# Prompt tiles' residual sums moved to ScalarE and GpSimd, prompt picks moved to rounds 11 to 14, weight loads placed behind the exchange, in a two-layer diffusion backbone

## The reference

```
mod = silu(cond) @ w_ada + b_ada                 # shift, scale, gate, twice; one row for prompt, one for sample
h   = rmsnorm(x) * (1 + sc1) + sh1
mix = [latent attention | gated conv | chunked gating MLP](h) @ w_out
x   = x + g1 * mix                               # the residual sum of this study
h   = rmsnorm(x) * (1 + sc2) + sh2
aff = softmax(h @ w_router)                      # 16 experts
gates, idx = top_k(aff.T, 2 * n / 16)            # each expert picks 32 prompt and 128 sample tokens
x   = x + g2 * scatter_add(gates * swiglu_expert(h[idx]))
```

## Time and profile before

| | us |
|---|---|
| median of 3 runs | 2421.12 (2415.95 to 2424.13) |
| the profiled execution, device time | 2425.75 |
| its span, first to last instruction | 2424.0 |
| PE busy | 2295.1 (95%) |
| DVE busy | 783.2 (32%) |
| ACT busy | 514.2 (21%) |
| POOL busy | 380.1 (16%) |
| mean granted TensorE clock | 0.969 of full |

### The profile page before, as it was taken

How to read it: one execution, slowest core, us unless ns; L and a number is a source line. 1 busy time by engine, 2 the same in 40 slices (tenths; PEclk the granted TensorE clock), 3 DMA queues, 4 the chain that set the end, 5 groups by cost and what they waited for, 6 DMA issues and landing times.

```text
span 2424.0 us, 29991 instructions
## 1 busy us (share of the span) xinstructions
PE 2295.1 (95%) x12052; PEld 1496.4 (62%) x12052; DVE 783.2 (32%) x1444; ACT 514.2 (21%) x1050; POOL 380.1 (16%) x540
## 2 busy tenths in 40 slices
PE   6999989989998899999999999899999959999996
PEld 4545545555545787887865455456554447887785
DVE  2401245444237312111234012456533461211213
ACT  3310122222234200110033101223223330010012
POOL 3000010011000322322310000120000022332221
PEclk8999999999999899999999999999999969999998
DMA  9100168778355788988970002685642258898898
GB/s 337 35 0 22 44 162 175 159 160 184 111 181 194 266 282 280 287 289 283 335 239 27 15 7 74 142 195 126 135 124 88 86 212 286 282 284 282 281 290 308
DMA packets 217657, 440.71 MB, mean 182 GB/s; under 512 B 33665, under 2 KB 76857, under 8 KB 217569
## 3 DMA queue, kind: packets, MB, share of 16 engines
q1 hardware_dynamic: 169200, 360.28, 46.7%
q0 software_dynamic: 24560, 54.57, 9.6%
q10 hardware_dynamic: 23808, 24.66, 4.9%
HBM read 339.34 MB, written 47.65 MB: 160 GB/s over the span
## 4 chain that ended last, share of the span: by engine, by line
PE 86%; DMA 6%; DVE 4%; SPq 2%; ACT 1%; issue 1%; ACTq 0%; DVEq 0%; POOLq 0%
PE PS L1417 11%; PE PS L1249 11%; PE PS L1424 11%; PE PS L1446 9%; PE PS L1031 9%; PE PS L1181 6%; PE PS L985 6%; PE PS L1124 5%; PE PS L972 5%; DMA r<-ring 4%; PE PS L1136 3%; PE PS L1440 2%; PE PS L1085 1%; SPq L563 1%; PE PS L939 1%; DMA ring<-in_w_down_dram 1%
## 5 line engine op out<-in xcount | busy, mean ns | idle before, releaser
L1417 PEld LDWEIGHTS PS<-r,ring 128*128 128x128 f32 x2048 | 285.5, 192 | 20.1 <-issue 18.3
L1417 PE MATMUL PS<-r,ring 128*128 128x160 f32 x2048 | 287.8, 302 | 4.8 <-ACT r L1737 3.8
L1249 PE MATMUL PS<-ring,mix 128*128 128x512 f32 x640 | 287.8, 597 | 0.0
L1424 PE MATMUL PS<-r,ring 128*128 128x160 f32 x2048 | 283.4, 299 | 0.0
L1424 PEld LDWEIGHTS PS<-r,ring 128*128 128x128 f32 x2048 | 279.9, 190 | 0.0
L1446 PE MATMUL PS<-ring,r 128*128 128x512 f32 x496 | 221.1, 599 | 0.0
L1031 PE MATMUL PS<-r,ring 128*128 128x512 f32 (+1 forms) x576 | 208.4, 521 | 1.6 <-ACT r L1538 1.6
L1124 PE MATMUL PS<-lat,r 128*128 128x512 f32 (+1 forms) x416 | 190.3, 593 | 7.7 <-ACT ring L1600 5.0
L1249 PEld LDWEIGHTS PS<-ring,mix 128*128 128x128 f32 x640 | 116.9, 190 | 128.1 <-issue 127.9
L1181 PE MATMUL PS<-r 128*128 128x256 f32 x768 | 177.0, 388 | 15.2 <-DMA r<-ring 15.2
L1181 PEld LDWEIGHTS PS<-r 128*128 128x128 f32 x768 | 149.4, 195 | 50.8 <-DMA r<-ring 18.0
(11 more groups left out here) (306 smaller groups left out, 2236.3 us busy)
## 6 DMA issues: line engine op xcount, KB each, us to landing
ring<-in_w_gate_dram SPq DMA_DIRECT2D x32, 2048.0 KB, 10.3
ring<-in_w_up_dram SPq DMA_DIRECT2D x32, 2048.0 KB, 10.1
ring<-in_w_down_dram SPq DMA_DIRECT2D x31, 2048.0 KB, 9.2
ring<-in_w_ada_dram SPq DMA_DIRECT2D x15, 2048.0 KB, 10.4
r<-ring SPq DMA_DIRECT2D x144, 96.0 KB, 5.5
r<-r SPq DMA_DIRECT2D x128, 96.0 KB
r<-r ACTq DMA_DIRECT2D x128, 96.0 KB
r<-ring ACTq DMA_DIRECT2D x112, 96.0 KB, 5.0
```

The costliest lines, as they stand in the source:

```text
L1249: ins = pe.matmul(psum(2 * (s % 2) + n, 512), mix[:, k, tile * P:(tile + 1) * P], W_OUT[n][:, k, :], start=(k == 4), stop=(k == 3))
L1417: ins = pe.matmul(PS[:, b // 2, (b % 2) * 256:(b % 2) * 256 + SLOTS], W_G[:, k, b * P:(b + 1) * P], XST[par][:, k, :], start=(k == 0), sto ...
L1424: ins = pe.matmul(PS[:, 2 + b // 2, (b % 2) * 256:(b % 2) * 256 + SLOTS], W_U[:, k, b * P:(b + 1) * P], XST[par][:, k, :], start=(k == 0), ...
```

## The change

Six edits, made together:

1. SP in the attention: the exchange of an item is issued first, then the weights of piece i+2, then its bias.
2. The prompt tiles' residual sums leave DVE. ACT copies each half of the projection from PSUM into `XO` (`copy_prompt_sums`), POOL multiplies it by the gate and adds the old rows (`add_prompt_residual`: four operations of 128x512 for each tile, each waiting for the one before).
3. Prompt picks in rounds 11 to 14 (`PROMPT_ROUND = 11`), and other places for the small prompt steps between the rounds.
4. The prompt tables are read by DVE after round 15 and not after round 12, so `idx_q` (and POOL's `XQ` gathers) come after the sample's last round. The semaphore `ptab_turned` is merged into `top_turned`.
5. `XQ_BANK = (0, 2, 4, 6)`: each of the four transposed prompt tiles has its own two PSUM banks, PE no longer waits for ACT between them, and the merge's last matmuls write banks 4 to 7.
6. The final load of the two prompt tiles moves from SP's queue to POOL's, straight behind the last prompt scatter.

```diff
-PROMPT_ROUND = 8
-XQ_BANK = (4, 6, 2, 4)
+PROMPT_ROUND = 11
+XQ_BANK = (0, 2, 4, 6)
...
+                    exchange(n, (0, 1) if n < NI - 1 else range(4))
                     if i >= 0:
                         load_ada_weights(i + 2)
-                    exchange(n, (0, 1) if n < NI - 1 else range(4))
-                    if i >= 0:
                         load_ada_bias(i + 2)
...
-            sp.wait_ge(yp_added, 16 * E * DEPTH + 16)
-            load_final(0)
...
+                def add_prompt_residual(s):
+
+                    pool.wait_ge(xd_landed[s % 2], at(l, 16 * NT // 2, 16 * (s // 2 + 1)))
+                    pool.wait_ge(xo_ready, at(l, NT, s))
+                    for n in range(2):
+                        c = slice(512 * n, 512 * (n + 1))
+                        pool.wait_ge(po_copied, at(l, 2 * PT, 2 * (s - NT + PT) + n + 1))
+                        pool.tensor_tensor(XO[s % 2][:, c], XO[s % 2][:, c], g1[:, 0, c], ALU.mult).then_inc(pool_own, 1)
+                        pool.wait_ge(pool_own, at(l, 4 * PT, 4 * (s - NT + PT) + 2 * n + 1))
+                        ins = pool.tensor_tensor(XO[s % 2][:, c], XO[s % 2][:, c], XD[s % 2][:, c], ALU.add)
+                        ins.then_inc(pool_own, 1)
+                    pool.wait_ge(pool_own, at(l, 4 * PT, 4 * (s - NT + PT) + 4))
+                    pool.sem_inc(xo_ready, 1)
...
+                    pool.wait_ge(yp_added, 16 * E * DEPTH + 16)
+                    pool.dma_start(mix_flat[:, 0:D * PT].rearrange("p (t d) -> p t d", t=PT),
+                                   x_dram[0:PT * P, :].rearrange("(t p) d -> p t d", p=P)).then_inc(fx_landed[0], 16)
...
                 def turn_prompt_rows(q):
                     pe.wait_ge(xq_landed[q], at(l, 16, 16))
-                    if q == 0:
-                        pe.wait_ge(h2_ready, at(l, 2 * NT, 2 * NT))
-                    if q == 1:
-                        pe.wait_ge(ptab_ready, at(l, 1, 1))
                     if q == 2:
-                        pe.wait_ge(xo_ready, at(l, NT, NT))
-                    if q == 3:
-                        pe.wait_ge(xsp_ready, at(l, 3, 1))
+                        pe.wait_ge(route_ready, at(l, 1, 1))
...
+                def copy_prompt_sums(s):
+
+                    act.wait_ge(xo_stored[s % 2], at(l, 16 * NT // 2, 16 * (s // 2)))
+                    act.wait_ge(h2_turned, at(l, NT, s - 1))
+                    act.wait_ge(xn2_ready, at(l, NT, s - 1))
+                    for n in range(2):
+                        act.wait_ge(out_summed, at(l, 2 * NT, 2 * s + n + 1))
+                        act.activation(XO[s % 2][:, 512 * n:512 * (n + 1)], psum(2 * (s % 2) + n, 512), ACT.Copy)\
+                            .then_inc(po_copied, 1)
...
-                add_residual(NT - 2)
                 dve.wait_ge(afft_ready, at(l, len(ROUTED), 4))
-                rounds(0, 2, 2 * E)
+                rounds(0, 3, 2 * E)
                 normalise_sums(NT - 2)
-                rounds(2, 4, 2 * E)
+                rounds(3, 5, 2 * E)
                 row_maxima(NT - 2)
-                add_residual(NT - 1, 0, D // 2)
+                rounds(5, 6, 2 * E)
                 affinity(NT - 2)
-                rounds(4, 5, 2 * E)
-                add_residual(NT - 1, D // 2, D)
-                rounds(5, PROMPT_ROUND - 1, 2 * E)
+                rounds(6, 9, 2 * E)
                 normalise_sums(NT - 1)
+                rounds(9, 10, 2 * E)
                 row_maxima(NT - 1)
                 largest(PROMPT_ROUND - 1, 2 * E)
                 affinity(NT - 1)
...
-                rounds(PROMPT_ROUND + 4, PROMPT_ROUND + 5, 2 * E)
-                dve.wait_ge(ptab_turned, at(l, 1, 1))
+                rounds(PROMPT_ROUND + 4, 16, 2 * E)
+                dve.tensor_scalar(top_f[0:2 * E, CAP_P:SLOTS], top_i[0:2 * E, CAP_P:SLOTS], half_base[:, :], None, ALU.add)\
+                    .then_inc(top_ready, 1)
+                dve.wait_ge(top_turned, at(l, 4, 1))
                 dve.tensor_copy(idx_q[:, :], PS[:, 7, 0:4])
                 dve.tensor_scalar(idx_p[:, :], PS[:, 7, 16:16 + E], 4.0, jcol[:, :], ALU.mult, ALU.add)
                 dve.tensor_copy(gate_p[:, :], PS[:, 7, 32:32 + E]).then_inc(ptab_ready, 1)
-                rounds(PROMPT_ROUND + 5, 16, 2 * E)
...
```

More of the change, by code:

```diff
@@ L377, in backbone @@
         p_turned = sem("p_turned")
+        po_copied = sem("po_copied")
         pt_landed = [sem(f"pt_landed{i}") for i in range(2)]
@@ L404, in backbone @@
         top_turned = sem("top_turned")
-        ptab_turned = sem("ptab_turned")
+        pool_own = sem("pool_own")
         ptab_ready = sem("ptab_ready")
@@ L779, in _ @@
                 spread_inverses(NI - 1)
+                def add_prompt_residual(s):
[10 more added lines that the diff above has]
+                    pool.sem_inc(xo_ready, 1)
+                for s in range(NT - PT, NT):
+                    add_prompt_residual(s)
                 pool.wait_ge(ptab_ready, at(l, 1, 1))
@@ L1335, in prompt_tables @@
                                         start=True, stop=True)
-                    ins.then_inc(ptab_turned, 1)
+                    ins.then_inc(top_turned, 1)
                 unit_landed(l, "out0")
@@ L1394, in _ @@
                     .then_inc(top_turned, 1)
+                pe.wait_ge(h2_ready, at(l, 2 * NT, 2 * NT))
+                pe.wait_ge(ptab_ready, at(l, 1, 1))
                 pe.wait_ge(lists_ready, at(l, 2, 2))
@@ L1398, in _ @@
                     for j in range(4):
-                        ins = pe.matmul(PS[32 * j:32 * j + 32, g, 64:64 + E], ident[own, own], merge[own, 1, :],
+                        ins = pe.matmul(PS[32 * j:32 * j + 32, 4 + g, 64:64 + E], ident[own, own], merge[own, 1, :],
                                         start=True, stop=True)
@@ L1403, in _ @@
                 turn_prompt_rows(1)
-                pe.wait_ge(route_ready, at(l, 1, 1))
                 turn_prompt_rows(2)
-                pe.wait_ge(xsp_ready, at(l, 3, 2))
                 turn_prompt_rows(3)
@@ L1721, in _ @@
                         normalise_prompt_sums(s - 1)
+                    if NT - PT <= s < NT:
+                        copy_prompt_sums(s)
                     if s < NT:
@@ L2074, in affinity, with add_residual @@
                     dve.tensor_scalar(out, logit[:, i, :], pinv[:, i:i + 1], None, ALU.mult).then_inc(aff_ready, 1)
[L2076 to L2091, removed]
+                def add_residual(s):
+                    dve.wait_ge(out_summed, at(l, 2 * NT, 2 * s + 2))
+                    dve.wait_ge(xd_landed[s % 2], at(l, 16 * NT // 2, 16 * (s // 2 + 1)))
+                    if s >= 2:
+                        dve.wait_ge(xo_stored[s % 2], at(l, 16 * NT // 2, 16 * (s // 2)))
+                        dve.wait_ge(ss2_ready, at(l, NT, s - 1))
+                        dve.wait_ge(h2_turned, at(l, NT, s - 1))
+                    step(dve.tensor_tensor(XO[s % 2], psum_wide(2 * (s % 2), D), g1[:, 1, :], ALU.mult))
+                    dve.tensor_tensor(XO[s % 2], XO[s % 2], XD[s % 2], ALU.add).then_inc(xo_ready, 1)
                 def normalise_sums(s):
@@ L2166, in _ @@
                 dve.tensor_copy(gate_p[:, :], PS[:, 7, 32:32 + E]).then_inc(ptab_ready, 1)
-                rounds(PROMPT_ROUND + 5, 16, 2 * E)
-                dve.tensor_scalar(top_f[0:2 * E, CAP_P:SLOTS], top_i[0:2 * E, CAP_P:SLOTS], half_base[:, :], None, ALU.add)\
-                    .then_inc(top_ready, 1)
-                dve.wait_ge(top_turned, at(l, 3, 1))
+                dve.wait_ge(top_turned, at(l, 4, 2))
                 dve.tensor_copy(lists[:, :, :], PS[:, 0, 0:4 * E].rearrange("p (v e) -> p v e", v=2)).then_inc(lists_ready, 1)
                 dve.wait_ge(lists_ready, at(l, 2, 1))
-                dve.wait_ge(top_turned, at(l, 3, 2))
+                dve.wait_ge(top_turned, at(l, 4, 3))
                 dve.tensor_tensor(gate_s[:, :], lists[:, 0, 0:E], PS[:, 1, 0:E], ALU.max)
@@ L2181, in _ @@
                 dve.tensor_scalar(idx_s[:, :], merge[:, 1, :], float(NP), None, ALU.add)
-                dve.wait_ge(top_turned, at(l, 3, 3))
-                dve.tensor_scalar(idx_4[:, 0:E, :], PS[:, 0:4, 64:64 + E].rearrange("p g e -> p e g"), 4.0, jcol[:, :],
+                dve.wait_ge(top_turned, at(l, 4, 4))
+                dve.tensor_scalar(idx_4[:, 0:E, :], PS[:, 4:8, 64:64 + E].rearrange("p g e -> p e g"), 4.0, jcol[:, :],
                                   ALU.mult, ALU.add).then_inc(route_ready, 1)
```

## The result

The changed kernel takes 2441.99 us (median of 9 runs, 2438.77 to 2447.76), the kernel before in the same job 2424.13. The ratio is 1.0073, 95% interval 1.0052 to 1.0094: **slower by 0.7%**, where I forecast 1.1% faster. The profiled execution has a span of 2445.3 us against 2424.0.

The account below looks back on a forecast made before the run. PE holds most of the span's end, so gains come only where PE waits. -35.5 + (0.9 + 4.5) + (0.9 + 3.5) - 1.5 = -27.2, span 2396.8, median 2394 us; range 2379 to 2410 (8 in 10).

Parts of the forecast that it names:

- Edit 1, -35.5: Attention: PE's waits for exchanged blocks and slow matmuls behind them go, 28.5 us in layer 0, 7.0 in layer 1; bounds 28, 38.
- Does all of it go?: Attention: step arguing from item 11, where blocks already precede 2 MB of weights without such a wait, that 35.5 us go.
- stays in part, at the second prompt exchange or by new waits: Rival, attention: the exchange's wait stays in part, half of 35.5 us, giving 2411 us; chance 0.05.
- Layer 1's 7.0: Attention, layer 1, first two pieces: waits of 1.31 and 2.82 us, plus 1.8 and 1.1 of slow matmuls, gained.
- the cover of 26 us: Attention: weights come some 6 us later, but their piece is multiplied over 26 us away, so PE does not wait.
- Edits 2 and 3, +0.9 a layer: Routing: with sums moved to ACT and POOL, DVE's last round ends 0.9 us later; bounds 4.6 earlier, 7.1 later.
- 785.2 + 8p: Routing: time in us when the last round ends; p is one POOL operation, taken as 1.1 us, giving 794.0.
- 14.6 + 4p: Routing: time in us from tile 8's root to tile 9's, with p one POOL operation, taken as 1.1 us.
- the rival with 1.87: Rival, routing: DVE holds POOL off, an operation takes 1.87 us, gathers at their ceiling: 2411 us in all; chance 0.14.
- Edit 4, +4.5 and +3.5: Last round to first expert: prompt gathers issued later make the expert start 4.5 us later in layer 0, 3.5 in layer 1.
- 2 to 5 late: Layer 0, before the first expert: the last late piece makes the merge start 2 to 5 us late; POOL's queue hides 2.4.
- half of its 7.9: Final load: the bound of -4 us, if its transfer beside the stores takes half of 7.9 us; -1.5 was taken.

Follow-up runs that it names:

- The form with late weights: The kernel before with edits 3 and 4, sums kept on DVE, and SP held until DVE begins round 11 before the late weights: 2427.01 us, single run.
- after_half_pool: The changed kernel without the multiplication by the gate, so POOL does two operations for each prompt tile and not four: 2427.89 us, single run.
- after_e1_item1: The changed kernel with the weights ahead of the exchange again at item 0 alone: 2417.03 us, ratio 0.9971 to the kernel before.

## Why the prediction was wrong

- **Edit 1, -35.5, measured -3.4 in the two profiles and nothing alone (ratio 1.0006).** The step that failed is "Does all of it go?", in two sentences. "The next item's blocks stand behind those 2 MB in the new order as they do there" took items 11 and 13, which are sample items with blocks of 1536 bytes, for the prompt items. And "only one of the two 2 MB loads is now ahead of it", at "7 us a load", counted every load as 7 us wherever it stands. The runs show that the place matters: the first load used to run at 312 GB/s in a gap and cost the exchange nothing. Turned behind the first exchange, it falls into a stretch of 8 us in which it moves at 32 GB/s, and is still in front of item 1's blocks; the next load then runs into item 2's. With item 0 alone left as it was, edit 1 gains 1.06%, 25.7 us. I had named the place as the tight one, and as a rival ("stays in part, at the second prompt exchange or by new waits") with a chance of 0.05 and half the gain. It took all.
- The price of the waits was right in layer 0 and not in layer 1. With the weights first at item 0 alone layer 0 gives 25.6 of its 28.5. Layer 1's 7.0 were read off one execution: the old order takes 225.9 to 226.5 us there in six other traces, the new one 226.4, so there was nothing to gain, and my lower bound of 28 for both would not have held (25.7 by the ratio). Waits for weights at the piece, which I excluded by the cover of 26 us, did not come.
- **Edits 2 and 3, +0.9 a layer, measured +5.2 and +4.8.** The mechanism was right, its size off. By 785.2 + 8p, p = 1.26 gives 795.3, 2.2 later. The other 3 lie in the path from root to root, 22.7 us (746.2 to 768.9) where 14.6 + 4p gives 19.6: DVE waits 1.87 us for PE's logits, since PE too stands for POOL's sum (2.80 us at 742.33) and its projection of 8 takes 5.29 us behind that; and from POOL's end to the root are 4.9 instead of 3.9, since PE's eight transposes, which ACT's copies wait for, take 1.97 behind PE's stop of 5.66 where the same eight took 1.09 at 742.33. I counted what DVE waits for and not what PE waits for.
- The Trainium skill's price (GPSIMD Engine Reference, section 3.1) gave an estimate of 1.12 by a quarter of its figure; measured are 1.26. Its rule of the shared port (SBUF — State Buffer, Who interferes with whom), by which the picks hold POOL off only at few moments, agrees: POOL's sixteen operations beside the picks take 1.255 to 1.268 us, so the rival with 1.87 is out.
- **Edit 4, +4.5 and +3.5: alone +2.8 and +3.5.** Right in layer 1, in part by luck: 3.7 us are DVE's stop ahead of `idx_4`, which I did not have, while the gathers themselves land sooner (5.2 to 5.5 us against 7.1 to 10.7) because the weights are through by then. In the whole change it is +6.3 and +6.8: the other 3.3 in layer 1 come from the first expert's weights, 7 us later in SP's queue behind tile 9's late rows. I had written that they come late and put no price on it. In layer 0 it is the last late piece, the effect of "2 to 5 late": the merge starts 6.3 later behind the round, and POOL's queue hides none of it.
- **Edit 5, nothing.** Not tried alone. The form with late weights has all of the routing's end but edit 5 and stands at 20.0 and 20.5 us from round to expert, the changed kernel at 20.1 and 20.5. Two other traces with edit 5, `after_half_pool` and `after_e1_item1`, have 20.8 to 21.5, so it gains nothing that shows; whether it costs up to 1 stays open.
- **Edit 6, -1.5: nothing.** The load's wait is for the scatter's landing (8.3 us) in either order. Alone, it starts 1.3 sooner, as the shorter queue says, and takes 1.65 longer beside the stores; that turns over my assumption "half of its 7.9".
- **The sum.** Of the 48.5 us between forecast and trace 32 lie in the attention, 13.4 in the routing (8.2 of it the relay, 5.1 the late weights and piece), 2.5 at the end. The step at item 0 is 29 of the 32 (491.6 us for both attentions against 462.5 with item 0 as it was; 25.0 by the medians). By the medians the whole gap is 45. Without the step at item 0 the change is 0.3% faster.

## What to carry to other kernels

When two transfers on one queue change places, ask of each in which stretch of time it will run and how fast that stretch is, not how many bytes it has: here the bulk load goes first where it can run in an idle gap, and behind the small blocks where it would hold them up. Turn such an order place by place; one that was right at the other places where weights are loaded lost all of its gain at item 0. Read the price of a wait off more than one execution: one of the two layers had no such wait in six of seven traces. Work taken off the busiest engine pays only if the relay that replaces it is shorter than the work it may hide behind, for every engine in the relay, and whatever is queued behind the relay's end (here the next stage's weights) has a price too.

## What was not expected of the hardware

- For some 8 us around the second prompt exchange whatever was in the queues moved slowly: 32 GB/s for a load alone, in packets of some 0.43 us, where the same kind of load had 0.09 us a packet and 342 GB/s just before (and 378 just behind) the stretch. The cause stays open.
- The exchange in blocks of 256 bytes moved 87 GB/s with the engines 0.48 busy, so the engines were not what it waited for. The Trainium skill (DMA: Bandwidth & Descriptors, Why small descriptors are slow) says that transfers from SBUF to SBUF don't suffer from small descriptors. That fits only in part: ACT's half of these blocks, 0.26 MB, took 18.2% of 16 engines' 7 us, by which a byte cost some 1.7 times what it cost in the load of 330 to 334 above (an estimate from these rows).
- Two loads of 2 MB issued 2 us apart ahead of such blocks held SP's issuing for 22 us, and PE for 19.
- DVE's write of an index table waited 3.6 to 3.7 us while POOL issued indirect gathers, and began 0.8 to 0.95 us behind the issue of the fourth. Eight other small instructions of DVE ran beside the same gathers without a wait, so the port rule named above doesn't settle which resource it was; that stays open.
- Indirect gathers of 512 KB landed 5.2 to 5.6 us after issue with no weights beside them (engines' share 0.8), 7.1 to 10.7 beside the expert's weights (1.03 to 1.04).
